# Two adaLN modulation blocks per PSUM bank, row copy and turn

## The reference, cut to what matters

```python
for l in range(DEPTH):
    mod_l = jnp.split((jax.nn.silu(c) @ ada_w[l] + ada_b[l])[:, None, :], 6, axis=-1)
    mod_c = jnp.split(jax.nn.silu(c_ctx) @ ada_w[l] + ada_b[l], 6, axis=-1)
    hl = modulate(rmsnorm(xl, norm_mix_pre[l]), mod_l[0], mod_l[1])
    hc = modulate(rmsnorm(xc, norm_mix_pre[l]), mod_c[0], mod_c[1])
    zl, zc = hl @ w_in[l], hc @ w_in[l]
    # ... four branches, merge ...
    xl = xl + mod_l[2] * rmsnorm(m_l, norm_mix_post[l])
    f_l = conv_ffn(modulate(rmsnorm(xl, norm_ffn_pre[l]), mod_l[3], mod_l[4]), ...)
    xl = xl + mod_l[5] * rmsnorm(f_l, norm_ffn_post[l])
```

## Time and profile before

| | us |
|---|---|
| median of 3 runs | 1653.98 |
| lowest, highest | 1651.18, 1657.06 |
| the profiled execution | 1649.58 |
| its span in the profile | 1647.8 |
| PE busy | 1590.0 (96%) |
| DVE busy | 932.1 (57%) |
| ACT busy | 789.6 (48%) |
| POOL busy | 309.6 (19%) |

### The profile page before, as it was taken

One profiled execution on the slowest core, in us unless ns is written; L12 is line 12 of the kernel. 1 busy time (PEld: TensorE's weight loads), 2 busy tenths in 40 slices (PEclk: granted clock), 3 DMA queues, 4 the chain that ended last, 5 costly groups with the idle time before them and its releaser, 6 DMA issues.

```text
span 1647.8 us, 33059 instructions
## 1 busy us (share of the span) xinstructions
PE 1590.0 (96%) x14076; PEld 1323.8 (80%) x14076; DVE 932.1 (57%) x1481; ACT 789.6 (48%) x1299; POOL 309.6 (19%) x248
## 2 busy tenths in 40 slices
PE   8999999998899999999999999999989899999998
PEld 6788767777678887888888886987877789889987
DVE  5364455564465569655554225655776265677764
ACT  4322456473354266443443225525766344566653
POOL 0160234323110000212222000312352120012210
PEclk9999999999999999999999999999999899999999
DMA  9753334233852352322225343833413295555453
GB/s 332 201 164 102 101 105 160 75 103 96 268 201 89 107 193 76 103 96 84 98 69 111 105 125 125 262 128 116 147 52 130 55 317 169 187 172 180 164 189 133
DMA packets 213840, 234.41 MB, mean 142 GB/s; under 512 B 5888, under 2 KB 194688, under 8 KB 213696
## 3 DMA queue, kind: packets, MB, share of 16 engines
q1 hardware_dynamic: 194208, 191.14, 35.3%
q0 software_dynamic: 14880, 34.87, 7.9%
q10 hardware_dynamic: 4608, 6.29, 1.1%
HBM read 216.55 MB, written 15.73 MB: 141 GB/s over the span
## 4 chain that ended last, share of the span: by engine, by line
PE 70%; DVE 3%; issue 3%; ACT 3%; DMA 1%; POOL 0%; ACTq 0%; DVEq 0%; POOLq 0%
PE ps L2333 15%; PE ps L2335 15%; PE ps L2334 15%; PE ps L2795 2%; PE ps L2629 2%; PE ps L2641 2%; PE ps L2424 1%; PE ps L2681 1%; PE ps L2398 1%; PE ps L2399 1%; PE ps L2400 1%; PE ps L2603 1%; PE ps L2788 1%; PE ps L2790 1%; PE ps L2789 1%
## 5 line engine op out<-in xcount | busy, mean ns | idle before, releaser
L1062 ACT ACTIVATE whi<-ring 128x1024 fp32r<-128x1024 f32 (+1 forms) x262 | 274.4, 1052 | 488.7 <-PE ps L2335 428.2
L1607 DVE TENSOR_TENSOR wlo<-ring,whi 128x1024 fp32r<-128x1024 f32 (+1 forms) x262 | 327.4, 1254 | 176.2 <-ACT whi L1062 175.4
L2333 PE MATMUL ps<-H,whi 128*128 128x256 f32 (+1 forms) x640 | 214.7, 336 | 1.8 <-DVE wlo L1607 1.8
L2335 PE MATMUL ps<-H,wlo 128*128 128x256 f32 (+1 forms) x640 | 214.2, 335 | 0.0
L2334 PE MATMUL ps<-H,whi 128*128 128x256 f32 (+1 forms) x640 | 214.2, 335 | 0.0
L2333 PE MATMUL ps<-HR,whi 128*128 128x512 f32 (+1 forms) x568 | 202.1, 356 | 0.5 <-DVE wlo L1607 0.3
L2335 PE MATMUL ps<-HR,wlo 128*128 128x512 f32 (+1 forms) x568 | 198.3, 349 | 0.0
L2334 PE MATMUL ps<-HR,whi 128*128 128x512 f32 (+1 forms) x568 | 198.2, 349 | 0.0
L2333 PEld LDWEIGHTS ps<-H,whi 128*128 128x128 f32 x640 | 121.5, 190 | 14.0 <-issue 1.9
L2335 PEld LDWEIGHTS ps<-H,wlo 128*128 128x128 f32 x640 | 121.5, 190 | 12.3
L2334 PEld LDWEIGHTS ps<-H,whi 128*128 128x128 f32 x640 | 121.5, 190 | 12.2
(11 more groups left out here) (399 smaller groups left out, 3219.2 us busy)
## 6 DMA issues: line engine op xcount, KB each, us to landing
ring<-in_ffn_up SPq DMA_DIRECT2D x44, 1024.0 KB, 5.0
ring<-in_w_gate SPq DMA_DIRECT2D x32, 1024.0 KB, 5.7
ring<-in_ada_w SPq DMA_DIRECT2D x32, 1024.0 KB, 5.3
ring<-in_w_in SPq DMA_DIRECT2D x24, 1024.0 KB, 7.9
ring<-in_ffn_down SPq DMA_DIRECT2D x10, 1024.0 KB, 5.0
ring<-in_ffn_down SPq DMA_DIRECT2D x18, 512.0 KB, 3.6
ada<-in_ada_w SPq DMA_DIRECT2D x8, 1024.0 KB, 11.6
WB<-in_w_branch POOLq DMA_DIRECT2D x8, 1024.0 KB, 6.3
```

Source lines behind the costliest of these rows:

```text
L1062: act.activation(whi[HALF_SLOT[m]][:, 0:kn, :], ring_half(raw, half, kn), ACT.Copy).then_inc(hi_done, 1)
L1607: dve.tensor_tensor(wlo[HALF_SLOT[m]][:, 0:kn, :], ring_half(raw, half, kn), whi[HALF_SLOT[m]][:, 0:kn, :].bitcast(F32), ALU.subtract).the ...
L2333: pe.matmul(o[:, c0:c1], hi[:, i, :], part(0, k), start=(k == 0), stop=False)
L2335: last = pe.matmul(o[:, c0:c1], lo[:, i, :], part(0, k), start=False, stop=(k == kn - 1))
```

## The change

The blocks are made in pairs. The first block of a pair (`mod`) uses the stationary columns 2 and 3, the second (`mod2`) the columns 0 and 1, by reading `cpad` two columns further on or not; both add up in one PSUM bank. One row copy takes both, one turn (`modt`) with a `fold` of four columns turns both, and DVE adds two biases. In the chunk steps one pair takes two steps: `mod` behind `cu` of step c, `mod2` behind `ch` of step c, the turn behind `cu` of step c + 1. Pairs stand at c = 1, 3, 5 in layer 0 and c = 1, 3 in layer 1. Attention has two pairs in layer 0 (unit steps 8 and 20, turns at 12 and 24; it was five blocks) and one in layer 1 (it was one block). `gap` 1 and 2 have a pair each, and their turns move into the up projection behind tile 4. The end of layer 0 has two pairs (it was three blocks); the gap before layer 1's projection has one pair (it was one block), whose turn moves behind the fourth z tile. In the ring, round the start of layer 1, the order is now: blocks (1,4), (1,5), (1,6), (1,7), `w_in` pair 6, pair 7, blocks (1,8), (1,9), `w_in` pairs 0, 1, 2. The ring keeps three slots. The diagonals and row jobs of the last projection move back by some tiles.

```diff
-CONST_COLS = [("ones", P), ("fold", 2), ...
+CONST_COLS = [("ones", P), ("fold", 4), ...
-TURN_AT, ROW_AT = (3, 4, 5, 6), (8, 9)
+TURN_AT, ROW_AT = (3, 4, 5, 6), (12, 14)
...
+def pair_jobs(pair):
+    return [("mod",) + pair[0], ("mod2",) + pair[1]], [("modt",) + pair[0]]
+TURN_Z, TURN_UP = 3, 4
+CHUNK_FILL = {0: (1, 3, 5), 1: (1, 3)}
...
+ATT_FILL = {0: (8, 20), 1: (4,)}
 def fill_plan():
-    before = [("att", 0, i) for i in (4, 10, 16, 22, 28)] + chunks(0) \
-        + [("gap", 0, 1)] * 2 + [("gap", 0, 2)] * 2 + [("end", 0, 0)] * 3
-    after = [("gap", 1, 0), ("att", 1, 4)] + chunks(1) + [("gap", 1, 1)] * 2 + [("gap", 1, 2)] * 2
...
+    for q, pair in enumerate(FIRST_PAIRS):
+        plan["start", 0, q] = sum(pair_jobs(pair), [])
+    rest = {0: iter(paired(MOD_BEFORE)), 1: iter(paired(MOD_AFTER))}
+    for l in range(2):
+        if l:
+            products, turns = pair_jobs(next(rest[l]))
+            plan["gap", l, 0], plan["z", l, 0] = products, turns
+        for i in ATT_FILL[l]:
+            plan["att", l, i], plan["att", l, i + 4] = pair_jobs(next(rest[l]))
+        for d in range(2):
+            for c in CHUNK_FILL[l]:
+                products, turns = pair_jobs(next(rest[l]))
+                plan["chunk", l, d, c, 0], plan["chunk", l, d, c, 1] = products[:1], products[1:]
+                plan["chunk", l, d, c + 1, 0] = turns
+        gaps = [pair_jobs(next(rest[l])) for _ in range(2)]
+        plan["gap", l, 1], plan["gap", l, 2] = gaps[0][0], gaps[1][0]
+        plan["up", l, 0] = gaps[0][1] + gaps[1][1]
+        if l == 0:
+            ends = [pair_jobs(next(rest[l])) for _ in range(2)]
+            plan["end", l, 0] = ends[0][0] + ends[1][0] + ends[0][1] + ends[1][1]
...
-        cpad = sb("cpad", [P, KT, STRIP])
+        cpad = sb("cpad", [P, KT, STRIP + 2])
...
 # ACT
-            def fill(point, part=slice(None)):
-                for job in [job for job in FILL.get(point, []) if job[0] == "mod"][part]:
+            def fill(point):
+                for job in [job for job in FILL.get(point, []) if job[0] == "mod2"]:
+                    s = filled(act, job)
...
                     for c in range(NCH):
-                        fill(("chunk", l, d, c))
+                        fill(("chunk", l, d, c, 1))
...
-                    fill(("gap", l, 2), slice(0, 1))
+                    fill(("gap", l, 2))
...
-                        if i == 0:
-                            fill(("gap", l, 2), slice(1, None))
 # DVE
+                        s = filled(dve, job)[:, 0:8].rearrange("p (x i s) -> p i x s", x=2, i=2)
+                        pair = PAIR_OF[job[1:]]
+                        for i, (_, n) in enumerate(pair):
+                            b = vc(l, "ada_b", 2 * n, 2).unsqueeze(2).to_broadcast([P, 2, 2])
+                            ins = dve.tensor_tensor(mod[:, l, 2 * n:2 * n + 2, :], s[:, i, :, :], b, ALU.add)
+                        ins.then_inc(frees(job), 1)
...
                     norm_apply(l, 0, X, Z, HR)
-                    fill(("gap", l, 0))
...
+                    if n == TURN_Z + 1:
+                        fill(("z", l, 0))
...
+                    if j == TURN_UP + 1:
+                        fill(("up", l, 0))
+                        gains(l, (3,))
 # PE
+                        second = name[0] == "mod2"
+                        c = cpad[:, :, 0:STRIP] if second else cpad[:, :, 2:2 + STRIP]
                         for k in range(KT):
                             g = k % STRIPS
-                            last = pe.matmul(o[STRIP * g:STRIP * g + STRIP, 0:SLOT_N], cpad[:, k, :], w[:, k, :],
-                                             start=(k < STRIPS), stop=(k >= KT - STRIPS))
+                            last = pe.matmul(o[STRIP * g:STRIP * g + STRIP, 0:SLOT_N], c[:, k, :], w[:, k, :],
+                                             start=(k < STRIPS and not second), stop=(k >= KT - STRIPS and second))
...
                         for x in range(2):
-                            last = pe.matmul(o[:, 2 * x:2 * x + 2], row[:, P * x:P * x + P], K("fold", 2),
+                            last = pe.matmul(o[:, 4 * x:4 * x + 4], row[:, P * x:P * x + P], K("fold", 4),
                                              start=True, stop=True)
...
                             done(last)
-                            fill(("chunk", l, d, c), "mod")
+                            fill(("chunk", l, d, c, 0))
...
                             done(last)
-                            fill(("chunk", l, d, c), "modt")
+                            fill(("chunk", l, d, c, 1))
...
+                    if n == TURN_Z:
+                        fill(("z", l, 0))
...
+                    if name[2:] == (TURN_UP, 1):
+                        fill(("up", l, 0))
```

More of the change, by code:

```diff
@@ L181, with paired @@
 MOD_AFTER = [(1, n) for n in range(8, 24)]
+def paired(blocks):
+    return [(blocks[n], blocks[n + 1]) for n in range(0, len(blocks), 2)]
+FIRST_PAIRS = [((0, q), (0, 4 + q)) for q in range(4)]
+MOD_PAIRS = FIRST_PAIRS + paired(MOD_BEFORE) + paired(MOD_AFTER)
+PAIR_OF = {b: pair for pair in MOD_PAIRS for b in pair}
+ATT_FILL = {0: (8, 20), 1: (4,)}
 def fill_plan():
-    def chunks(l):
-        return [("chunk", l, d, c) for d in range(2) for c in CHUNK_FILL[l]]
     plan = {}
-    for q in range(4):
-        pair = [(0, q), (0, 4 + q)]
-        plan["start", 0, q] = [(kind,) + b for kind in ("mod", "modt") for b in pair]
@@ L193, in fill_plan @@
-    before = [("att", 0, i) for i in (4, 10, 16, 22, 28)] + chunks(0) \
-        + [("gap", 0, 1)] * 2 + [("gap", 0, 2)] * 2 + [("end", 0, 0)] * 3
-    after = [("gap", 1, 0), ("att", 1, 4)] + chunks(1) + [("gap", 1, 1)] * 2 + [("gap", 1, 2)] * 2
-    for blocks, points in ((MOD_BEFORE, before), (MOD_AFTER, after)):
-        jobs = modulation_jobs(blocks)
-        assert len(points) == len(blocks)
-        for n, p in enumerate(points):
-            last = n == len(points) - 1
-            plan.setdefault(p, []).extend(jobs[max(0, 2 * n - 1):None if last else 2 * n + 1])
+    for q, pair in enumerate(FIRST_PAIRS):
+        plan["start", 0, q] = sum(pair_jobs(pair), [])
@@ L202, in fill_plan @@
+    assert not any(list(r) for r in rest.values())
     return plan
 FILL = fill_plan()
-MOD_GAP = [job[1:] for l in range(2) for k in (1, 2) for job in FILL["gap", l, k] if job[0] == "mod"]
+MOD_GAP = [job[1:] for l in range(2) for k in (1, 2) for job in FILL["gap", l, k]]
 GAP_SLOT = [g % (4 if g // 4 in FUSED else 2) for g in range(len(MOD_GAP))]
@@ L295, with product_of, turn_of @@
 JOB = job_list()
-MOD_NO = {job[1:]: n for n, job in enumerate(j for j in JOB if j[0] == "mod")}
+PAIR_NO = {job[1:]: n for n, job in enumerate(j for j in JOB if j[0] == "mod")}
+def product_of(block):
+    return ("mod" if PAIR_OF[block][0] == block else "mod2",) + block
+def turn_of(l, n):
+    return ("modt",) + PAIR_OF[l, n][0]
 PAIRED = {"LM1", "LM2", "ln", "sx", "sy", "xv", "u0", "ta", "at", "cu", "y1", "y23"}
@@ L302, in bank_plan, with share @@
     place, release, needs = {}, {}, {}
-    owner, count, g = [None] * NBANK, [0] * NBANK, 0
+    owner, count, g, turn = [None] * NBANK, [0] * NBANK, 0, 0
+    def share(name):
+        first = ("mod",) + PAIR_OF[name[1:]][0]
+        place[name], release[name], needs[name] = place[first], release[first], set()
     early = list(JOB)[:JOB["z", 0, Z_ORDER[0]]]
     for name in early:
-        k = NBANK - 2 + JOB[name] % 2
+        if name[0] == "mod2":
+            share(name)
+            continue
+        k = NBANK - 2 + turn % 2
+        turn += 1
         place[name] = k
@@ L2194, in _ @@
                     scaled_out(0)
-                    fill(("gap", l, 1))
                     new_x(0)
@@ L2404, in project_tokens, with fill @@
                             last.then_inc(w_used, 1)
-            def fill(point, kind=None):
+            def fill(point, kinds=("mod", "mod2", "modt")):
                 for name in FILL.get(point, []):
-                    if kind not in (None, name[0]):
+                    if name[0] not in kinds:
                         continue
-                    if name[0] == "mod":
+                    if name[0] != "modt":
                         if name[1:] in MOD_FIRST:
```

78 lines of the change are left out of this document (31 added, 47 removed).

## The result

| | before | after |
|---|---|---|
| median of ten runs each, side by side (us) | 1653.96 | 1659.19 |
| lowest, highest | 1651.18, 1659.26 | 1656.93, 1664.25 |
| profiled execution, its span | 1649.58, 1647.8 | 1658.86, 1657.0 |
| a second profiled execution, its span | 1657.03, 1655.2 | 1654.39, 1652.6 |
| PE busy, TensorE instructions | 1590.0, 14076 | 1585.3, 13980 |

The ratio is 1.0031, with a 95% interval of 1.0018 to 1.0045. The changed kernel is slower, by 5.2 us and not by the 12.7 forecast. The page and the groups by line show half the turns, and the products as before.

What follows compares the result with a forecast made beforehand. PE, 70% of the chain, was taken as the bound. Small terms +1.65, late block 4.5, late next load 4.9 and clock 1.65 made +12.7 on median 1653.98: 1666.7 us, own range 1662 to 1670, 8 in 10 1657 to 1674.

Steps and rivals of the forecast that it cites:

- the beginning of layer 1: From layer 0's end into layer 1's projection: block (1,9) late +4.5, next load late +4.9, one clock fall +1.65.
- Sum so far: +1.65: All terms outside layer 1's beginning: start -0.95, attention -2.1 and +0.5, chunk steps +3.1, gaps before the FFN +1.1.
- the fourth block of layer 0's end also has to wait for a slot: End of layer 0: its slot wait is covered by later splits; if they were not late, up to 4.8.
- The clock: Layer 1's beginning: idle PE brings one fall of the granted clock, +1.65, between 0 and two or three falls.
- Chunk pair, 5.47: Chunk loops: the turn waits for a fresh row copy, so two steps take 5.47 for 5.04, +0.4 a pair.
- rival 4: Slower still: two or three clock falls, +3.3, and one stall of 1 in each chunk loop, +4; 1674, 15%.
- Norms before the FFN: Gaps before the FFN: one row copy and no turn between products brings the second norm's root earlier, -0.5 a layer.
- Attention of layer 0: Five blocks and four turns become four blocks and two turns, with PE nearly always fed: -2.1.
- FFN turns: Up projection: four turns, two a layer, move in where nothing hides them, +2.1; DVE additions cost nothing.
- Rival 1: Layer 1's beginning: the ring is late only once, pair 0 nearly in time, no clock fall; +7.3, 1661.3, 17%.
- Rival 2: Layer 1's beginning: neither wait is on the path, something else holds the start; +1.65, 1655.6, 8%.
- Rival 3: Chunk steps: the copy lies ready, turns pay in full, a pair takes 4.51; 1646.6 if the ring keeps up, 5%.

Runs made afterwards that it cites:

- the variants run beside their own before: Four kernels, each the changed kernel with one edit: idle matmuls, chunk turns behind `ch`, FFN turns in the gap, branch load first; 1658.53, 1655.70, 1654.49, 1655.94 us.
- single blocks and a full edge: The kernel before, unpaired, with four blocks at layer 0's end and two before layer 1's projection, one fewer in each layer's attention; 1662.83 us, ratio 1.0052.
- the kernel with 2.08: The changed kernel with one pair at layer 0's end, none before layer 1's projection, and the two pairs moved into attention; 1654.84 us, ratio to before 1.0005.
- the late turn: The changed kernel with the turn of a chunk pair moved from behind `cu` to behind `ch` of the same step; 1655.70 us, ratio to before 1.0014.

## Why the prediction was right in its direction and wrong in its size

Forecast +12.7, measured +5.2. The terms for the beginning of layer 1 came near, 11.05 for 9.5 measured. What failed is the other part of the sum, "Sum so far: +1.65". It measured -4.3, the 5.2 of the medians less those 9.5: two stretches that have no term in it shrank by 2.9 and 2.45, the chunk steps cost 0.96 instead of 3.1, and layer 1's norm before the FFN shrank by 2.84 instead of 0.5.

**The beginning of layer 1: right in its path.** Forecast 4.5 + 4.9 + 1.65 = 11.05, measured 9.5 in the mean of two profiles each. The chain of releases (two splits, slot, load, product, row copy, `norm_finish`) is in the trace step by step. Sizes: the load took 5.1 rather than 4.8 (1016.19 to 1021.29). The Trainium skill, DMA: Bandwidth & Descriptors, section Measured, has 6.15 for 1 MB, for loads issued from GpSimd; this one, issued by SP, shows 1 less while it runs alone. Pair 0 took 6.57 (1038.84 to 1045.41), with POOL's store beside it. In tile 0's wait 2.64 to 2.77 is idle where 4.9 was forecast. Pair 0 goes out at the split of tile 15, as forecast, but that split, 1036.46 before, came only 2.4 later and not 4.5. To the wait come the turn, 0.5, and a fall of 1.7.

The idle time before the second product is 0.72, and not the 3 to 4 that I gave as a sign: the slow sums of squares fill it. With nine idle matmuls in the earlier wait it is 4.51.

One step of this part failed: "the fourth block of layer 0's end also has to wait for a slot, but [...] this is covered". It isn't: PE is idle for 4.45, and this is what brings the clock down. It didn't add up in time, since the (1,9) load covers what the clock costs and the other way round.

**The clock: mis-sized.** Forecast 1.65 in all. The table has 7.1 more lost in the mean, the variants run beside their own before 3.3 to 6.2. Most of it lies inside the 9.5 of the edge and isn't on top of it: the first 5.2 are in the trace 5.1 of lost work and hardly any idle time. So the term was too small as lost work, and the idle terms too large by as much.

**The small terms: this is where the size went wrong.** Without the beginning of layer 1 I had +1.65. By the medians it is 5.2 - 9.5 = -4.3, by the two profiles of each 3.4 - 9.5 = -6.1. Named by their steps:
- *Chunk pair, 5.47.* The step "ch to cu 1.04" was mis-sized. It was read from the first step of a loop, which isn't like the others: the state is made there by another instruction (line 2024, not 2027), and in the second loop the trace names ACT's copy of `AT` as what `cu` waited for. Inside the loop it is 359.20 to 359.99 = 0.79. With it my own sum gives 5.22, and 5.20 was measured. The loops cost +0.96 and not +3.1. The waiting turn with `ch` behind it is right in kind: the Trainium skill, TensorE: Matmul & The Clock Gate, section Step-by-step: what each phase is for, has matmuls in program order, and the trace agrees, `ch` is issued behind the turn.
- *What I didn't look at: the stretch behind the loops.* I had no term for it. The reading of the states is 2.9 shorter. In both profiles of before, PE stands still in it for 3.0 with nothing that the profile shows, and while a gate load runs:

```profile
439.33 6.94 SPq L838 DMA_DIRECT2D ring<-in_w_gate  x2
...
446.50 0.27 PE L2758 MATMUL ps<-LM,nu 64*64 64x64 f32 x2 [3.02 <-issue]
```

 It is there too with single blocks and a full edge (2.98), in neither profile of after, and in two of the paired kernels (2.08 and 0.99). The first profile of before has another in the first loop (2.50 at 379.34), and the kernel with 2.08 one of 1.29. The trace says more than that line. The DMA view lists single transfers of 16 KB of kind "instruction" on a queue of their own, q8. All seven of these stalls end 1.3 to 1.6 after such a transfer has ended (here 444.02 to 444.90, PE on at 446.50), and in both profiles of before and the kernels with 2.98 and 2.08 PE stops after the same number of records of matmuls and weight loads (10177, once 10178). So PE most likely waits there for its own next instructions. In the first profile of before the transfer begins 3.6 after the reading began, when the gate load's traffic thins out (the hardware queue has 108% of the DMA engines' time in 441 to 443.9, 34% in 443.9 to 445). In both profiles of after SP issues its last load of the loop earlier, 2.2 before the states are read (436.94 in the first) and not 1.1, the transfer begins 2.9 after the reading began, and nothing stalls. Two paired kernels have it at 3.6 and 3.8 without a stall; their PE runs at the slow clock there. All this is read from times; no run moved the transfer or the load, so the cause isn't shown.
- *The preparations of the chunk loops, no term either*: 2.45 shorter, and the clock accounts for all of it: 7.8 us of work lost in the mean of the two profiles of before, 4.3 in those of after. Whether the change removes them is open.
- *Blocks late in the second loop*: rival 4's stall exists. PE waits 1.24 and 1.66 in the two profiles of after for the last block of layer 0's second loop, and 0.45 in before. It is one of 1 to 2 in one loop, not 1 in each of four.

```profile
435.80 1.07 PE L2461 MATMUL ps<-ring,cpad 128*32 128x256 f32 x16 [1.24 <-DMA ring<-in_ada_w]
```

- *Norms before the FFN*: -0.67 in layer 0 as forecast (-0.5); in layer 1 at full clock 15.08 to 13.56 = -1.5, three times as much, and the rest of the -2.84 is one profile of before, 17.71 long, with a fall of the clock.
- *Attention of layer 0*: -1.15 for -2.1. The product counts in full, the turns hardly: two turns less are worth 0.15 here and not 1.06. PE was not as fed as I took it to be.
- *FFN turns*: 0.95 a layer as forecast (1.06), plus a fall of 1.7 in five of eight profiles. The additions on DVE cost nothing that shows.
- *Branch load of layer 1*: a new wait, 1.88 and 0.79 in the two profiles of after, costed at nothing. I had counted which queue the change moves, but not what a load then runs beside when two queues move against each other.

**The rivals.** Rival 1 came nearest in time (1661.3), by luck: both loads of the ring were late, which it denies. The small terms made up for it. Rival 2 is refuted by the kernel without the gap pair. Rival 3 falls with the late turn, since even without the copy's wait a pair is 5.01.

**The base.** I added my sum to the median and took the durations from an execution 4.4 below it. In it no work was lost at places where the second profile lost 2 to 4 (first loop, second norm before the FFN, second FFN). That doesn't explain the 7 us by itself, but it shows that terms below 2 can't be read off one pair of profiles.

## What to carry to other kernels

When work is regrouped, count slots, not engine time: a pair that needs two ring slots where one was free turned a hidden 1 MB load into 9.5 us, and moving that one pair took the whole loss away. Two waits that cover each other must be removed together, and an experiment that takes away one of them shows which is behind. And read the latency of a chain from the middle of its loop, from several places, not from its first step. Stretches to which a sum gives no term should be compared first: here two of them moved by 5.4 together, more than the measured difference.

## What the runs showed of the hardware that I had not expected

- During a wait of 4.45 us on PE the granted clock fell to half of 2.4 GHz for some 10 us (0.57 over 12 us), so that the sums behind it took 9.80 us. Nine matmuls of no use in the wait kept the full clock (1.00 instead of 0.57), and gained nothing, since a load was late as well.
- The mean granted clock of an execution went with the kernel: about 19 us of work lost in the kernel before, 26 in the changed one, 24 in the unpaired one with the same ring order. Falls at the edge are in all profiles with that order, others come and go. Two executions of one kernel differed by 7.5 us.
- Two 1 MB loads issued 0.5 us apart took 8.4 and 10.9 us. The first of them took 5.9 when the other waited for it, and lone 1 MB loads of SP took 4.8 and 5.1.
- PE stood still for 3.0 us between small matmuls with nothing that the profile names, in all three profiles of kernels with single blocks, and went on 1.4 to 1.6 us after a 16 KB transfer of instructions had ended.
